# A third work item on each half of the tokens at the inner norms of a two-layer encoder

## The reference

```python
h = rms_norm(x, mix_pre_norm[l]);  proj = h @ w_in[l]          # 1024 x 1952
groups = [norm(hyena FFT convolution), norm(GQA, 8 heads), norm(MLA, 4 heads)]
x = x + rms_norm(groups @ w_out[l], mix_post_norm[l])
h = rms_norm(x, ffn_pre_norm[l]);  up = dwconv3(h @ w_up[l])   # 1024 x 5632
f = (gelu(gate) * val) @ w_down[l]                             # 2816 x 1024
x = x + rms_norm(f, ffn_post_norm[l])
```

## Time and profile before

| | |
|---|---|
| three runs | 1461.18, 1466.32, 1467.24 us (median 1466.32) |
| profiled execution | 1464.45 us, its span 1462.6 us |
| TensorE | busy 1382.0 us, 94% |
| VectorE, ScalarE, GpSimd | 63%, 40%, 38% |
| mean granted TensorE clock | 0.990 |

### The profile page before, as it was taken

How to read it: one execution, slowest core, us unless ns; L and a number is a source line. 1 busy time by engine, 2 the same in 40 slices (tenths; PEclk the granted TensorE clock), 3 DMA queues, 4 the chain that set the end, 5 groups by cost and what they waited for, 6 DMA issues and landing times. The chain is left out here.

```text
span 1462.6 us, 15399 instructions
## 1 busy us (share of the span) xinstructions
PE 1382.0 (94%) x5940; PEld 1027.0 (70%) x5940; DVE 924.8 (63%) x992; ACT 587.0 (40%) x864; POOL 552.2 (38%) x287
## 2 busy tenths in 40 slices
PE   7999988988999999999989998988989999999998
PEld 5587654367788888788866785433768888887886
DVE  6776875456788778711186778655477787884113
ACT  5322454444534344432252226444354434343223
POOL 3222332026444443444552215220364444444443
PEclk9999999999999999999999999999999999999999
DMA  7312301012333333233331222100222333333332
GB/s 250 87 29 65 81 11 33 0 44 72 87 90 97 96 92 100 80 97 101 98 131 56 58 55 48 29 15 1 84 61 86 102 88 99 94 90 95 94 92 85
DMA packets 205538, 112.53 MB, mean 77 GB/s; under 512 B 15303, under 2 KB 202425, under 8 KB 204570
## 3 DMA queue, kind: packets, MB, share of 16 engines
q1 hardware_dynamic: 205466, 111.54, 26.2%
HBM read 105.63 MB, written 2.10 MB: 74 GB/s over the span
## 5 line engine op out<-in xcount | busy, mean ns | idle before, releaser
L509 POOL TENSOR_TENSOR wl<-raw,wh 128x1024 fp32r<-128x1024 f32 x176 | 430.9, 2450 | 702.2 <-ACT wh L588 702.1
L588 ACT ACTIVATE wh<-raw 128x1024 fp32r<-128x1024 f32 x176 | 186.4, 1060 | 560.9 <-PE ps L1095 528.6
L1093 PE MATMUL ps<-gh,wh 128*128 128x512 f32 (+1 forms) x864 | 346.5, 401 | 5.3 <-POOL wl L509 5.3
L1095 PE MATMUL ps<-gh,wl 128*128 128x512 f32 (+1 forms) x864 | 341.6, 395 | 0.0
L1094 PE MATMUL ps<-gl,wh 128*128 128x512 f32 (+1 forms) x864 | 341.5, 395 | 0.0
L1093 PEld LDWEIGHTS ps<-gh,wh 128*128 128x128 f32 (+1 forms) x864 | 161.9, 187 | 49.3 <-issue 9.4
L1094 PEld LDWEIGHTS ps<-gl,wh 128*128 128x128 f32 (+1 forms) x864 | 161.8, 187 | 40.6 <-issue 1.9
L1095 PEld LDWEIGHTS ps<-gh,wl 128*128 128x128 f32 (+1 forms) x864 | 161.8, 187 | 39.3
L1537 DVE TENSOR_TENSOR acc<-acc,sq 128x512 f32<-128x512 f32 x24 | 60.6, 2525 | 191.0 <-ACT sq L632 190.8
L1967 DVE SCALAR_TENSOR_TENSOR cv<-pad,pm,cv 128x512 f32<-128x512 f32 x88 | 130.7, 1485 | 77.6 <-ACT cv L952 77.6
L1093 PE MATMUL ps<-fh,wh 128*128 128x512 f32 x308 | 121.7, 395 | 0.7 <-POOL wl L509 0.7
(11 more groups left out here) (274 smaller groups left out, 2211.9 us busy)
## 6 DMA issues: line engine op xcount, KB each, us to landing
raw<-w_up SPq DMA_DIRECT2D x88, 512.0 KB, 3.8
raw<-w_down SPq DMA_DIRECT2D x32, 512.0 KB, 3.8
raw<-w_in SPq DMA_DIRECT2D x30, 512.0 KB, 4.0
raw<-w_out SPq DMA_DIRECT2D x16, 512.0 KB, 4.1
raw<-w_down SPq DMA_DIRECT2D x16, 384.0 KB, 3.3
xio<-x SPq DMA_DIRECT2D x4, 512.0 KB, 4.0
win<-c_win SPq DMA_DIRECT2D x2, 1024.0 KB, 5.5
TF<-c_tf SPq DMA_DIRECT2D x2, 1024.0 KB, 8.7
```

What stands on the lines that cost most here:

```text
L509: nc.gpsimd.tensor_tensor(l, raw[:, slot, :], h.bitcast(F32), ALU.subtract).then_inc(S["lo_ready"], 1)
L588: A(xh[:] if third(lay, n) else wh[:, slot, :], raw[:, slot, :], ACT.Copy).then_inc(S["hi_ready"], 1)
L1093: mm(ps[0:cols, bank, :], w_hi, x_hi, start=start and k == 0, stop=False)
L1095: ins = mm(ps[0:cols, bank, :], w_lo, x_hi, start=False, stop=stop and k == tile_n - 1)
```

## The change

At the three inner norms `first_pair` becomes `first_three`: items 0, 1 and 2 of the following matrix run on each chunk of a half. The third one's weights come from a fourth pair of buffers (`Z`: `zh`, `zl`, with a raw buffer of their own), filled by `fourth`, `fourth_hi` and `fourth_lo` at other places of the queues than before; the item after it takes `xh` and `xl`. For that a fifth y is saved to SBUF, the second halves' first steps on VectorE stand before the first half's last two `gl`, `x_stat` moves to a later item, the up projection rotates over six banks in place of four, the input projection's W3 goes to bank 7, and the filter's taps and spectra move by about one item.

```diff
+FOURTH = [I_UP + 2, ITEMS + 2, ITEMS + I_UP + 2]
 def third(lay, n):
     lay, n = lay + n // ITEMS, n % ITEMS
-    return n in (2, I_OUT + DC - 1, I_UP + 2, ITEMS - 1)
+    return n in (I_OUT + DC - 1, I_UP + 3, ITEMS - 1) or n == (3 if lay else 2)
 def freed(lay, n):
     lay, n = lay + n // ITEMS, n % ITEMS
     g = lay * ITEMS + n
-    if n in (I_OUT + DC - 1, ITEMS - 1, I_UP + 1, I_UP + 4, 4) or (lay > 0 and n == 1):
+    if n in (I_OUT + DC - 1, ITEMS - 1, I_UP + 1, I_UP + 3, I_UP + 4, I_UP + 5, 4) or (lay > 0 and n in (1, 3, 5)):
         return g - 1
-    if n in (2, I_UP + 2):
+    if n == 2:
         return g
     return g + 1
+def split(lay, n):
+    g = lay * ITEMS + n
+    return g + 1 - sum(z <= g for z in FOURTH)
...
-        ysave = probT0
+        ysave = [[probT0[:, m, :] for m in range(4)] + [y4] for y4 in (vg[:].rearrange("p s n -> p (s n)"), gact[:])]
+        Z = [(zraw[:], zh0[:], zl0[:]), (pad[:, :, 1:T + 1], zh1[:], zl1[:])]
         groot = [rbc[:], cv[:, 1, :], rbc[:]]
...
-        LAST_BANK = [(DC - 1, 1), (DC - 1, 3)]
+        LAST_BANK = [(DC - 1, 1), (DC - 1, 4)]
         LAG = 4
-        W_BANK = [0, 1, 3] + [(t - 3) % 2 for t in range(3, WIN - 2)] + [4, 5]
+        W_BANK = [0, 1, 3, 7] + [t % 2 for t in range(4, WIN - 2)] + [4, 5]
+        UP_BANK = lambda j, k: 2 + 2 * (j % 3) + k
+        TAP_BANK = [4, 4, 6, 4]
         ROOT_BANK = [2] * 6 + [6]
...
                     item(lay, I_OUT + i, w_out[bass.ds(lay, 1), :, :, i * P:(i + 1) * P])
+                sp.wait_ge(S["mlo"], lay * 4 + 4)
+                sp.wait_ge(S["mk_in"], (lay + 1) * 16 * MH)
+                fourth(0, w_up[lay:lay + 1, :, :, P:2 * P])
                 for i in range(4, DC - 1, 2):
                     for j in range(2):
...
                 for m in range(0, DC - 1, 2):
+                    if m == 2 and lay < DEPTH - 1:
+                        sp.wait_ge(S["f_conv"], (lay + 1) * 2 * FC)
+                        fourth(1, w_in[lay + 1:lay + 2, :, :, 2 * P:3 * P])
...
                 for n in range(I_UP + 2, ITEMS + 1 if lay < DEPTH - 1 else ITEMS - 1, 2):
+                    if n == I_DOWN + 12 and lay < DEPTH - 1:
+                        fourth_lo(lay, 1)
                     for slot in range(2):
-                        lo(lay * ITEMS + n + slot, slot)
+                        if n + slot != I_UP + 2:
+                            lo(lay * ITEMS + n + slot, slot)
                 add(lay, 1)
...
+            def fourth_hi(lay, b):
+                act.wait_ge(S["z_in"], 32 * (2 * lay + b + 1))
+                A(Z[b][1], Z[b][0], ACT.Copy).then_inc(S["z_hi"], 1)
...
                 for c in range(DC):
-                    if c == 4:
-                        hi(lay, n + 1, 1)
+                    if c == 5:
+                        hi(lay, n, 0)
                     if c >= 2:
...
                 A(sq[:, m % 2, :], ps[:, m, :], ACT.Square).then_inc(S["ysq"], 1)
-                if m < 4:
-                    A(ysave[:, m, :], ps[:, m, :], ACT.Copy).then_inc(S["ycopy"], 1)
+                if m < 5:
+                    A(ysave[b][m], ps[:, m, :], ACT.Copy).then_inc(S["ycopy"], 1)
             def last_square(lay, b, half):
...
                 prep(q, off, 0, range(4, DC))
-                hi(lay, n, 0)
+                hi(lay, n, 1)
                 prep(q, off, 1, range(DC))
-                prep_squares(q, lay, n)
+                prep_squares(q, lay, n + 1)
                 prep_root(q)
...
                     ysquare(lay, 0, m)
+                    if m == 2:
+                        fourth_hi(lay, 0)
                 hi(lay, I_UP + 1, 1)
-                new_stream(lay, 0, I_UP + 2)
-                hi(lay, I_UP + 4, 0)
+                new_stream(lay, 0, I_UP + 3)
...
+                        if m == 3 and lay < DEPTH - 1:
+                            fourth_hi(lay, 1)
                 if lay < DEPTH - 1:
                     hi(lay, ITEMS + 1, 1)
-                    new_stream(lay, 1, ITEMS + 2)
+                    new_stream(lay, 1, ITEMS + 3)
                 C.join()
...
+            def first_three(lay, q, n, banks):
+                for i in range(3):
+                    item_ready(lay, n + i)
+                for half in range(2):
+                    for k in range(DC + 1):
                         if k < DC:
                             pe.wait_ge(S["gh_ready"], chunk(q, half, k))
                             pe.wait_ge(S["gl_ready"], chunk(q, half, k))
-                            first = triple(lay, n, k, banks[0], cols, gh, gl, k, k == 0, k == DC - 1)
-                            if k == DC - 1 and (half or not q):
+                            first = triple(lay, n, k, banks[0], HALF[half], gh, gl, k, k == 0, k == DC - 1)
+                            if k == DC - 1 and half:
                                 first.then_inc(S["pe_item"], 1)
-                        if k == DC - 2 and q == 0:
-                            pe.wait_ge(S["fw2_in"], 16 * DEPTH)
-                            pe.wait_ge(S["f_sin"], 1)
-                            filt_layer(1)
-                        if k == lag:
-                            item_ready(lay, n + 1)
-                        if k >= lag:
-                            second = triple(lay, n + 1, k - lag, banks[1], cols, gh, gl, k - lag, k == lag, k == DC + lag - 1)
-                second.then_inc(S["pe_item"], 1)
...
-                    b = 4 + 2 * (j % 2)
+                    if j == 1 or j == 3:
+                        pe.wait_ge(S["fc_done"], lay * 4 + j - j // 2)
+                    if j == 2:
+                        pe.wait_ge(S["evac"], lay * WIN + 4)
+                    b = TAP_BANK[j]
                     rows = slice(lay * HHID, (lay + 1) * HHID)
...
-                first_pair(lay, lay * 2, 0, (0, 1))
                 if lay == 0:
+                    first_pair()
                     parameters()
-                for t in range(2, WIN):
-                    if t == 2 and lay:
+                else:
+                    first_three(lay, lay * 2, 0, W_BANK)
+                for t in range(3 if lay else 2, WIN):
+                    if t == 3:
                         filt_taps(0)
-                    if t == 5:
+                    if t == 6:
                         filt_spec(2)
                         filt_spec(3)
-                    if t == 6:
-                        h_turn(0)
                     if t == 7:
                         h_forward(0)
...
-                pe.wait_ge(S["ycopy"], lay * 2 * 4 + 4)
+                pe.wait_ge(S["ycopy"], lay * 2 * 5 + 5)
                 last_item(lay, 0, I_OUT + DC - 1, DC, yh, yl, 0, True)
                 def gate_up(k):
-                    if k == 6:
+                    if k == 2:
                         x_stat(lay * 2 + 1)
-                first_pair(lay, lay * 2 + 1, I_UP, (2, 3))
+                first_three(lay, lay * 2 + 1, I_UP, (UP_BANK(0, 0), UP_BANK(0, 1), UP_BANK(1, 0)))
                 for j in range(1, FC):
                     for k in range(2):
-                        if j >= 2:
-                            pe.wait_ge(S["f_evac"], (lay * FC + j - 2) * 2 + k + 1)
-                        tiles(lay, j * 2 + (I_UP + k), k, 2 + 2 * (j % 2) + k, DC, gh, gl, 0, True, True,
-                              gate=gate_up if j == 1 and k == 0 else None)
+                        if j == 1 and k == 0:
+                            continue
+                        if j >= 3:
+                            pe.wait_ge(S["f_evac"], (lay * FC + j - 3) * 2 + k + 1)
+                        tiles(lay, j * 2 + (I_UP + k), k, UP_BANK(j, k), DC, gh, gl, 0, True, True,
+                              gate=gate_up if j == 2 and k == 0 else None)
...
                 q, off = lay * 2 + b + 1, (lay + b) * PML + PM["mix_pre" if b else "ffn_pre"]
-                for half in range(2):
-                    dve.wait_ge(S["rms_post"], (lay * 2 + b) * 2 + half + 1)
-                    for c in range(DC + 2):
-                        if c < DC:
-                            step(lay, b, c, half)
-                            if c == half == 0:
-                                own_add(lay, b, 0, 0, "x_new")
-                        if c >= 2:
-                            operand_lo(q, off, c - 2, half)
+                for i in range(2 * DC + 2):
+                    if i < 2 * DC:
+                        half, c = divmod(i, DC)
+                        if c == 0:
+                            dve.wait_ge(S["rms_post"], (lay * 2 + b) * 2 + half + 1)
+                        step(lay, b, c, half)
+                        if i == 0:
+                            own_add(lay, b, 0, 0, "x_new")
+                    if i >= 2:
+                        operand_lo(q, off, (i - 2) % DC, (i - 2) // DC)
             def last_stream(lay):
...
                     xsum(lay * 2)
-                    taps(0)
+                else:
+                    dve.wait_ge(S["const_ok"], 1)
+                taps(0)
```

(6 more changed lines are left out.)

129 lines of the change are left out of this document (87 added, 42 removed).

## The result

The changed kernel takes 1488.57 us (median of four, 1484.17 to 1489.06), the kernel before, timed beside it, 1465.42 (median of four, 1461.18 to 1467.24). The ratio is 1.0143, 95% interval 1.0119 to 1.0167: slower by 1.4%. The profiled execution took 1488.83 us, its span is 1487.0.

A forecast was written before the change was run, and what follows sets the result against it. TensorE, busy 94% of the span, was taken as the bound. Terms -2.0 + 1.5 + 8.1 + 0.4 + 8.8 = +16.8 us on 1464.45 gave 1481, stated as 1482, range 1469 to 1492.

The forecast's parts named there:

- third item's gain per norm: At each inner norm, the third item costs 0.4 us in place of 5.57, a gain of 5.2 us.
- wait at U5, twice: At both feed-forward norms, TensorE waits 5.4 us for the sixth up-projection item, its weight copy standing behind the gelu.
- D12's later start: First layer's thirteenth down-projection item: its split stands behind `zl`, which waits for `zh`, so it starts 8.1 us later.
- second mix's norm, W3's copy late: Norm into the second layer's mix: ScalarE waits 3.5 us for W3's weights, making the last `gl` 2.8 us later.
- third tap group: Second layer's mix: the third taps wait 3.9 us (2.5 to 4.5) for VectorE's fourth evacuation, of bank 7.
- the fifth y from SBUF: Fifth VectorE step at a norm reads y from SBUF, may wait for GpSimd's adds; counted as nothing, worst 1.8 us per norm.
- clock: TensorE drops to half clock after each of four new waits, 2.2 us each (0 to 3.3), +8.8 us in all.
- B (copies in time): ScalarE reaches the copies for the sixth up item and `zh` in time, removing 25.5 us: 1455.5; chance 0.08.
- C (D12's wait absent): Only the wait at the first layer's thirteenth down item is absent, 10.3 us less: 1471; chance 0.14.
- Rival A: TensorE's clock stays up through the new waits: 1472.5 us; chance 0.12.
- Rival D: At the norms VectorE, held by GpSimd, sets the pace, no third-item gain: 1487 us; chance 0.66 together with the forecast.
- What would show it: Profile signs: `gl` waits under 5 us, two `wl` waits about 5, one about 8, taps about 4, PEclk below 9 there.

The follow-up runs named there:

- e13_no_third: The changed kernel with six edits to late copies, loads and taps, but each norm's third item run whole behind the pair: 1475.95 us, ratio 1.0069.
- e9_best: The changed kernel with six edits: a split, two weight copies and W3's load earlier, second taps later, separate banks for the fourth tap group: 1460.48 us, ratio 0.9959.
- e4_raw3_taps: The changed kernel with W3's load issued ahead of the filter table and the second taps behind the fourth evacuation: 1481.44 us, ratio 1.0119.
- e10_warm: The changed kernel with 84 unread matmuls filling four of TensorE's waits, no copy, split or evacuation moved: 1476.33 us, ratio 1.0070.

## Why the prediction was right in direction and 7 us short

The measured 1488.6 lies in the range (1469 to 1492), above the forecast of 1482. By its own steps, in us:

| step | forecast | measured |
|---|---|---|
| third item's gain per norm | 5.2 | 5.0 (18.9 + 5.57 - 19.5, changed kernel); 5.1 (e13_no_third against e9_best: 15.2 over three stages) |
| wait at U5, twice | 5.4 | 5.53, 5.53 |
| norm 1 and 3 without the clock | -1.0 each | -0.9 at norm 3 (2.03 - 2.9) |
| norm 1 and D12 without the clock | +7.1 | 12.87 - 5.9 = +7.0 |
| D12's later start | 8.1 | a wait of 7.76 |
| second mix's norm, W3's copy late | 2.8 | 1.4 (24.5 us from first chunk to next item, 21.5 in e4_raw3_taps, less 1.6 of clock) |
| third tap group | 3.9 | 3.97 |
| second mix without the clock | +1.5 | 6.59 - 6.4 = +0.2 |
| first layer's start | +0.4 | 1.78 - 1.3 = +0.5 |
| the fifth y from SBUF | 0 | 0.9 at the last norm |
| **clock** | **+8.8** | **+16.5** |

The rows "without the clock" are what is left of a stage's growth when the clock's loss is taken off, so they are no tighter than a stage is.

**The waits** were read correctly from the changed order and the durations of before, the four long ones within 0.4 us. Only W3's late copy was put 1.4 us too high. Rivals B (copies in time) and C (D12's wait absent) fell with them.

**The step that was mis-sized is the clock.** "For each new wait I take 2.2, between that and twice it (3.3), bounds 0 and 3.3": the windows gave 2.9, 2.9, 3.0 and 4.8. Two places were not counted at all, the wait of 2.05 us behind W3's copy (1.6) and 1.3 at 314, where no new wait stands. The 7.7 us more make up the difference between the 1481.3 of the sum and the 1488.83 of the profiled execution: 2.6 at the taps, 2.9 at the two places, 2.2 at the other three. These last are partly luck, as the same waits cost less in other traces (last section). I had one row at half clock, behind a wait of 1.92, and carried its size to waits up to four times as long. Rival A (no fall) is refuted by the windows above and by e10_warm. The Trainium skill ("TensorE: Matmul & The Clock Gate", What's actually happening) says that activity releases the throttle: the unread matmuls agree at three of four places, and there it made no difference to the clock that nobody used the results.

**Rival D fits the time and is wrong.** It had VectorE set the pace, no gain from the third item, and 1487, closer to 1488.6 than my own forecast. The 19.5 us for three items and e13_no_third show the gain that it denies. Its closeness is luck too: it was priced at 2 us a norm, while no gain at all would have cost 5.2 at each, 1497 in all and outside the range. The time alone would have chosen the wrong cause.

**What would show it**: `gl` under 5 us in all was not met (7.1; 5.05 without the 2.05 of W3's late copy); PEclk below 9 showed in the slices of D12 and of the taps, but not in those of U5.

**A term counted at nothing** was the fifth step's y from SBUF. At the inner norms no effect of it is to be seen, as the forecast had it, since TensorE is behind there. At the last norm it isn't. First the changed kernel, then the kernel before:

```profile
1473.60 0.94 DVE L1642 SCALAR_TENSOR_TENSOR tb<-gact,pm,rr 128x256 f32<-128x256 f32 x1
1474.47 0.47 DVE L1642 SCALAR_TENSOR_TENSOR tb<-ps,pm,rr 128x256 f32<-128x256 f32 x1
```

```profile
1450.33 0.86 DVE L1558 SCALAR_TENSOR_TENSOR tb<-ps,pm,rr 128x256 f32<-128x256 f32 x2
```

0.94 instead of 0.47, twice, is 0.94 of the 1.1 us by which the last stage grew, and it grew in every kernel with the change. No run undid it, so it is read, not tested. SBUF alone doesn't do it: two steps from `probT`, which is in SBUF as well, took 0.88 us together at 1470.86 and 1.35 at 1471.99.

## What to carry to other kernels

Filling a stall of TensorE with more work gains that work only if everything behind it moves up too: here the third item gave about 5 us at every norm, and a copy, a split and a load that had just been in time each took more back. Read the changed order on the feeding engines (what stands ahead of the copy, behind what the copy waits) before counting the gain, and expect the next thing in line to be late once the first is mended. Count a new wait of 4 to 8 us on TensorE at its length and 1.5 to 3 us more for the clock (4.8 where the tap matmuls stood behind it). If it can't be removed, filling it with matmuls nobody reads got that part back at four of the five places where I tried it.
